# Long filters of a Hyena layer, transformed with the lags in eight residue classes of 128 instead of four of 256

## What is computed

```python
def hyena_filters(L, w1, b1, w2, b2, w3, b3, freq):
    ...
    h = (hid @ _f32(w3) + _f32(b3)).reshape(L, HY_ORDER, 2, HY_WIDTH)
    h = h * jnp.exp(-t * jnp.abs(deltas))[:, None, None, :]
    fwd, bwd = h[:, :, 0], h[:, :, 1]
    kern = jnp.concatenate([fwd, jnp.zeros((1, HY_ORDER, HY_WIDTH), jnp.float32), bwd[:0:-1]], axis=0)
    kern = kern / jnp.sum(jnp.abs(kern), axis=0, keepdims=True)
    return jnp.fft.rfft(kern, axis=0)

def long_conv(u, k_f, skip):
    L = u.shape[1]
    uf = _f32(u)
    y = jnp.fft.irfft(jnp.fft.rfft(uf, n=2 * L, axis=1) * k_f, n=2 * L, axis=1)[:, :L]
    return (y + uf * _f32(skip)).astype(u.dtype)
```

## Time and profile before

| what | value |
|---|---|
| median of three runs (lowest, highest) | 4657.28 us (4656.59, 4658.3) |
| the profiled execution, its own time | 4660.92 us |
| its span in the trace | 4658.4 us |
| TensorE (PE) busy | 4558.7 us, 98% |
| VectorE (DVE) busy | 2077.1 us, 45% |
| ScalarE (ACT) busy | 1006.0 us, 22% |
| GpSimd (POOL) busy | 44.8 us, 1% |
| granted TensorE clock, mean | 0.989 |

### The profile page before, as it was taken

The page is one execution under the profiler, slowest core; times in us unless marked ns, Lnnn a source line. Parts: engine busy times, 40 slices in busy tenths (PEclk is TensorE's granted clock), DMA queues, the critical chain, the costliest instruction groups (busy, mean ns, idle before and its releaser), DMA issues.

```text
span 4658.4 us, 39533 instructions
## 1 busy us (share of the span) xinstructions
PE 4558.7 (98%) x16516; PEld 2273.6 (49%) x16516; DVE 2077.1 (45%) x2485; ACT 1006.0 (22%) x1349; POOL 44.8 (1%) x35
## 2 busy tenths in 40 slices
PE   7999999998999999999999999999999999999998
PEld 3446666543444444554555554544444444444444
DVE  4555555224444477744344535323643362333412
ACT  3135555212111100002333222222310010000000
POOL 0000000000000000000000000000000000000000
PEclk9999999998999999999999999989999999999999
DMA  6200000211333422221111011112221221111211
GB/s 255 75 28 10 6 10 11 108 68 37 118 113 131 174 108 104 104 104 60 41 36 38 32 41 41 37 45 82 88 95 41 84 73 45 40 42 45 83 42 57
DMA packets 106813, 320.28 MB, mean 69 GB/s; under 512 B 26085, under 2 KB 44261, under 8 KB 99082
## 3 DMA queue, kind: packets, MB, share of 16 engines
q1 hardware_dynamic: 89708, 306.22, 18.6%
q10 hardware_dynamic: 16928, 11.54, 0.8%
HBM read 257.36 MB, written 60.36 MB: 68 GB/s over the span
## 4 chain that ended last, share of the span: by engine, by line
PE 70%; DVE 4%; issue 1%; DMA 0%; ACT 0%; POOL 0%; DVEq 0%; SPq 0%; POOLq 0%
PE late_dense L122 34%; PE late_four L3370 11%; PE late_two L3370 5%; PE late_four L1433 3%; PE late_four L3600 3%; PE late_four L2420 2%; PE late_dense L3600 2%; PE late_four L1445 1%; PE late_four L1450 1%; PE late_two L1625 1%; PE late_two L1631 1%; PE late_two L3600 1%; PE late_four L1649 1%; PE late_two L2774 0%; PE late_two L2776 0%
## 5 line engine op out<-in xcount | busy, mean ns | idle before, releaser
L122 PE MATMUL late_dense<-arena 128*128 128x512 f32 x4008 | 1764.7, 597 | 7.3 <-ACT arena L1758 2.9
L122 PEld LDWEIGHTS late_dense<-arena 128*128 128x128 f32 x4008 | 758.0, 191 | 934.9 <-issue 921.7
L3370 PE MATMUL late_four<-arena 128*128 128x512 f32 x1160 | 504.5, 592 | 0.0
L135 ACT ACTIVATE arena<-late_dense 128x512 f32<-128x512 f32 x198 | 118.0, 596 | 1112.5 <-PE late_dense L122 1084.6
L3370 PEld LDWEIGHTS late_four<-arena 128*128 128x128 f32 x1160 | 220.4, 190 | 277.4 <-issue 273.9
L122 PE MATMUL attn_dense<-arena 128*128 128x512 f32 x640 | 282.5, 599 | 4.0 <-ACT arena L637 2.1
L3370 PE MATMUL late_two<-arena 128*128 128x512 f32 x576 | 253.4, 592 | 0.0
L3419 DVE TENSOR_TENSOR arena<-late_four,arena 128x512 f32<-128x512 f32 x145 | 98.7, 689 | 299.3 <-PE late_four L3370 295.2
L839 PE MATMUL attn_dense<-matrices,arena 128*128 128x128 f32 x1280 | 187.6, 282 | 18.2 <-ACT arena L885 16.1
L122 PEld LDWEIGHTS attn_dense<-arena 128*128 128x128 f32 x640 | 121.7, 192 | 159.0 <-issue 154.4
L3370 PEld LDWEIGHTS late_two<-arena 128*128 128x128 f32 x576 | 109.4, 190 | 137.8 <-issue 136.3
(11 more groups left out here) (390 smaller groups left out, 4719.6 us busy)
## 6 DMA issues: line engine op xcount, KB each, us to landing
arena<-in_ada_w SPq DMA_DIRECT2D x12, 2048.0 KB, 8.1
arena<-in_w_ffn_in SPq DMA_DIRECT2D x44, 512.0 KB, 4.0
arena<-in_hy_tables SPq DMA_DIRECT2D x16, 1280.0 KB, 6.1
arena<-in_hy_w_in SPq DMA_DIRECT2D x32, 512.0 KB, 3.5
spectrum<-arena SPq DMA_DIRECT2D x8, 2048.0 KB, 8.0
arena<-spectrum SPq DMA_DIRECT2D x8, 2048.0 KB, 11.4
arena<-in_w_gates SPq DMA_DIRECT2D x32, 512.0 KB, 3.3
spill<-arena SPq DMA_DIRECT2D x26, 512.0 KB, 4.4
```

The costliest lines, as they stand in the source:

```text
L122: mm = pe.matmul(self.ps[:, n % SEG], self.wbuf[:, slot, k], job.rhs[:, k, cols], start=(job.first and k == 0), stop=(job.last and k == kt ...
L135: act.activation(job.out[:, cols], self.ps[:, n % SEG], job.func, scale=job.scale, bias=job.bias).then_inc(self.emptied[n % SEG], 1)
L3370: mm = pe.matmul(product_bank(M, name, i), left[:, k], right[:, k], start=(k == 0), stop=(k == 3))
```

## The change

The lags of the filters are ordered by residue modulo 8: eight classes of 128 lags, each one tile, and one tile of 128 base frequencies in place of two. For a base frequency the eight class results make eight frequencies, real and imaginary. Classes r and 8 - r (and 0 with 4, 2 with 6) are added in PSUM, with tables of both signs (`MINUS` lists the eight that are needed negated), so that each of four banks takes two matmuls. A step has four such groups of 8 matmuls (`filter_group_pe`): two on `minus`, which give the imaginary planes, then two on `plus` (the real ones). Each group is now read by `group_act` and `group_dve`, and `filter_spectrum_dve` joins the two groups of a part in eight planes; it has six instructions, two of them with the square root of one half. `n` counts these spectra as before, two a step, now by part and not by `f`. The store writes them back to the places that the signal part reads, in pieces of 512 numbers (2 KB). One table of 24 blocks of 128 by 128 (1.5 MB) is loaded once, ahead of the layer; the signal part's tables lose the negated part (1.25 MB to 1 MB), and the loads between filter steps fall away.

```diff
-            sp.dma_start(Y.tables.rearrange("p a b -> p (a b)")[:, 0:2 * L + BANK], A["hy_tables"][0]).then_inc(Y.early_in, 16)
+            sp.dma_start(Y.tables.rearrange("p a b -> p (a b)"), A["hy_filter_tables"]).then_inc(Y.early_in, 16)
...
+MINUS = ((COS, 4), (SIN, 7), (SIN, 6), (SIN, 5), (SIN, 4), (COS, 2), (COS, 1), (COS, 3))
+EVEN_LAGS = ((((COS, 4, 1), (COS, 0, 1)), ((COS, 4, -1), (COS, 0, 1)), ((COS, 2, 1), (COS, 6, 1)), ((SIN, 2, 1), (SIN, 6, -1))),
...
+def filter_group_pe(pe, Y, n, lags, rhs, fixed=0):
+    if n:
+        pe.wait_ge(Y.group_read, n)
+    for bank in (2, 3, 0, 1):
+        for at, (kind, r, sign) in enumerate(lags[bank]):
+            if fixed and bank == 0 and r == 0:
+                pe.wait_ge(Y.row_fixed, fixed)
+            mm = pe.matmul(Y.group[:, bank], filter_block(Y, kind, r, sign), rhs[:, r], start=(at == 0), stop=(at == 1))
     mm.then_inc(Y.group_filled, 1)
...
+def filter_spectrum_dve(dve, Y, n):
+    S, X, root = Y.S, Y.X, math.sqrt(0.5)
+    dve.wait_ge(Y.group_read, 2 * n + 2)
+    if n:
+        dve.wait_ge(Y.x_stored, 16 * n)
+    dve.tensor_tensor(X[:, 1], S[:, 5], S[:, 6], ALU.add)
+    dve.tensor_tensor(X[:, 3], S[:, 5], S[:, 6], ALU.subtract).then_inc(Y.d, 1)
+    dve.tensor_tensor(X[:, 0:4:2], S[:, 0:4:2], S[:, 4:8:3], ALU.add)
+    dve.tensor_tensor(X[:, 4:8:2], S[:, 0:4:2], S[:, 4:8:3], ALU.subtract)
+    dve.wait_ge(Y.d, 2 * n + 1)
+    dve.scalar_tensor_tensor(X[:, 5:8:2], X[:, 1:4:2], -root, S[:, 1:4:2], ALU.mult, ALU.add).then_inc(Y.d, 1)
+    dve.wait_ge(Y.d, 2 * n + 2)
+    dve.scalar_tensor_tensor(X[:, 1:4:2], X[:, 1:4:2], root, S[:, 1:4:2], ALU.mult, ALU.add).then_inc(Y.x_ready, 1)
...
         sp.wait_ge(Y.x_ready, n + 1)
-        sp.dma_start(A["spectrum"][n], Y.X).then_inc(Y.x_stored, 16)
+        it, real = divmod(n, 2)
+        dst = A["spectrum"][2 * it:2 * it + 2].rearrange("f p (s t) c -> t p s f c", t=2)[1 - real]
+        sp.dma_start(dst, Y.X.rearrange("p (s f) c -> p s f c", f=2)).then_inc(Y.x_stored, 16)
...
-        table(2 * it + 1)
         store_spectrum(2 * it)
         dense.load(sp, 4 * it + 4)
-        table(2 * it + 2)
+        if it == STEPS - 1:
+            table(0)
         store_spectrum(2 * it + 1)
...
             elif it:
-                pe.wait_ge(Y.x_ready, 2 * it)
+                pe.wait_ge(Y.group_read, 4 * it)
...
-        even_pe(pe, Y, 2 * it, Y.plus, Y.minus, it + 1)
+        filter_group_pe(pe, Y, 4 * it, EVEN_LAGS[1], Y.minus)
...
-        odd_lags_pe(pe, Y, 2 * it)
+        filter_group_pe(pe, Y, 4 * it + 1, ODD_LAGS[1], Y.minus)
...
-        even_pe(pe, Y, 2 * it + 1, Y.plus, Y.minus)
+        filter_group_pe(pe, Y, 4 * it + 2, EVEN_LAGS[0], Y.plus, it + 1)
         dense.multiply(pe, 1)
-        odd_lags_pe(pe, Y, 2 * it + 1)
+        filter_group_pe(pe, Y, 4 * it + 3, ODD_LAGS[0], Y.plus)
...
-        for f in range(2):
-            s = 2 * it + f
-            group_dve(dve, Y, s, 0)
-            if not f:
+        for real in range(2):
+            n = 2 * it + real
+            if n:
+                dve.wait_ge(Y.x_ready, n)
+            group_dve(dve, Y, 2 * n, 0)
+            if not real:
                 conv(4 * it)
-            if s:
-                dve.wait_ge(Y.x_stored, 16 * s)
-            dve.wait_ge(Y.group_filled, 2 * s + 2)
-            dve.wait_ge(Y.group_read, s + 1)
-            spectrum_dve(dve, Y, group[:, 0:2], group[:, 3:1:-1])
-            if not f:
+            group_dve(dve, Y, 2 * n + 1, 1)
+            filter_spectrum_dve(dve, Y, n)
+            if not real:
                 conv(4 * it + 1)
```

More of the change, by code:

```diff
@@ L1370, in __init__ @@
         self.ring, self.u, self.turned = rows[:, 17:19], rows[:, 19:21], rows[:, 21:23]
-        tables = self.tables = rows[:, 45:48].rearrange("p a b -> p (a b)")[:, 0:2 * L + BANK]
-        self.table = tables[:, 0:2 * L].rearrange("p (r s k c) -> p r s k c", r=CLASSES, s=2, k=2)
-        self.table_minus = tables[:, 2 * L:2 * L + BANK].rearrange("p (s k c) -> p s k c", s=2, k=2)
+        tables = rows[:, 45:48].rearrange("p a b -> p (a b)")
+        self.filter_table = tables.rearrange("p (n c) -> p n c", c=P)
+        self.tables = tables[:, 0:2 * L]
+        self.table = self.tables.rearrange("p (r s k c) -> p r s k c", r=CLASSES, s=2, k=2)
         self.plus, self.minus = pieces(23, 4), pieces(27, 4)
@@ L1411, in ring_row, with pair_pe @@
         return self.ring[:, self.ring_use[name] % 2]
-def even_pe(pe, Y, s, first, second, fixed=0):
-    if s:
[L1418 to L1431, removed]
+def pair_pe(pe, Y, s, odd, rhs):
+    pe.wait_ge(Y.table_in, 16 * (s + 1))
+    for a, r in enumerate((odd, odd + 2)):
+        for part in range(2):
             for k in range(2):
@@ L1435, in pair_pe, with filter_block, group_act @@
     mm.then_inc(Y.group_filled, 1)
[L1438 to L1451, removed]
+def filter_block(Y, kind, r, sign):
+    return Y.filter_table[:, LT * kind + r if sign > 0 else 2 * LT + MINUS.index((kind, r))]
+def filter_group_pe(pe, Y, n, lags, rhs, fixed=0):
[6 more added lines that the diff above has]
+            mm = pe.matmul(Y.group[:, bank], filter_block(Y, kind, r, sign), rhs[:, r], start=(at == 0), stop=(at == 1))
     mm.then_inc(Y.group_filled, 1)
-def group_act(act, Y, n, filled):
-    act.wait_ge(Y.group_filled, filled)
+def group_act(act, Y, n):
+    act.wait_ge(Y.group_filled, n + 1)
     if n:
@@ L1535, in hyena_sp @@
             at += 2
-        table(2 * STEPS + 2 * j + 1)
+        table(2 * j + 1)
         dense.load(sp, at)
@@ L1541, in hyena_sp @@
         if 2 * j + 2 < 8:
-            table(2 * STEPS + 2 * j + 2)
+            table(2 * j + 2)
         dense.load(sp, at + 3)
@@ L1691, in first_pair @@
         o, half = ROUNDS[j]
-        s, n, z = 2 * STEPS + 2 * j, 2 * STEPS + 4 * j, Y.z[half]
+        s, n, z = 2 * j, 4 * STEPS + 4 * j, Y.z[half]
         if o == 0:
@@ L1696, in first_pair @@
             pe.wait_ge(Y.inv_read, 8 * (half + 1))
-        pe.wait_ge(Y.group_read, n) if j else pe.wait_ge(Y.x_ready, s)
-        pair_pe(pe, Y, s, 0, z, z)
+        pe.wait_ge(Y.group_read, n)
+        pair_pe(pe, Y, s, 0, z)
     first_pair(0)
     for j, (o, half) in enumerate(ROUNDS):
-        s, n, z = 2 * STEPS + 2 * j, 2 * STEPS + 4 * j, Y.z[half]
+        s, n, z = 2 * j, 4 * STEPS + 4 * j, Y.z[half]
         dense.multiply(pe, 1)
         pe.wait_ge(Y.group_read, n + 1)
-        pair_pe(pe, Y, s, 1, z, z)
+        pair_pe(pe, Y, s, 1, z)
         dense.multiply(pe, 1)
@@ L1772, in hyena_act @@
             turn_act(act, Y, 4 * it - 1)
+        group_act(act, Y, 4 * it + 1)
+        if it:
             turn_act(act, Y, 4 * it)
@@ L3926, in hyena_arrays @@
     tokens = 4 * np.arange(LT // CLASSES * P).reshape(1, -1, P) + np.arange(CLASSES).reshape(-1, 1, 1)
-    by_class = tokens.reshape(-1)
-    angles = np.pi / L * np.multiply.outer(tokens, np.arange(2 * P) + 0.5)
+    shifted = np.concatenate([np.arange(P), 2 * P + np.arange(P)])
+    angles = np.pi / L * np.multiply.outer(tokens, shifted + 0.5)
     waves = np.stack([np.cos(angles), -np.sin(angles)], axis=1).astype(np.float32)
     tables = waves.reshape(CLASSES, 2, 2, P, 2, P).transpose(4, 3, 0, 1, 2, 5)
-    tables = np.concatenate([tables.reshape(2, P, -1), -tables[:, :, 3].reshape(2, P, -1)], axis=2)
+    eighths = LT * np.arange(P) + np.arange(LT).reshape(-1, 1)
+    by_class = eighths.reshape(-1)
+    angles = np.pi / L * np.multiply.outer(eighths, np.arange(P) + 0.5)
+    blocks = np.stack([np.cos(angles), -np.sin(angles)]).astype(np.float32)
+    minus = np.stack([-blocks[kind, r] for kind, r in MINUS])
+    filter_tables = np.concatenate([blocks.reshape(2 * LT, P, P), minus]).transpose(1, 0, 2)
     back_tables = waves.reshape(CLASSES, 2, 2 * P, 2, P).transpose(4, 3, 0, 1, 2).reshape(P, -1)
```

37 lines of the change are left out of this document (21 added, 16 removed).

## The result

| what | before | after |
|---|---|---|
| median of four runs (lowest, highest) | 4657.79 us (4656.59, 4659.83) | 4611.49 us (4610.95, 4615.45) |
| the profiled execution, its own time | 4660.92 us | 4615.45 us |
| its span | 4658.4 us | 4613.4 us |
| TensorE busy | 4558.7 us | 4511.3 us |
| VectorE busy | 2077.1 us | 2106.8 us |

The ratio is 0.9901, with a 95% interval of 0.9889 to 0.9912: 46.3 us faster, where 57.5 were forecast. The time, 4611.5, lies above the range that ended at 4608. VectorE gained 30 us of busy time and ScalarE 8, as the counts say (32 and 8 were forecast).

The account below looks back on a forecast made before the run. The prediction took TensorE as the bound, on the chain for 70% of the span. Removed matmuls (54.9 us) plus shorter table waits (2.6) made 57.5 us less, from 4657.3 to 4599.8 us, range 4596 to 4608.

Parts of the forecast that it names:

- The matmuls removed: Filter part's transform: 128 records of 0.429 us go over four steps, 54.9 us less, all on the path.
- The joins between groups: Between a step's filter groups: banks are free 3.6 us after a group, covers leave at least 3.3 us, cost nothing.
- the fear of one rival: In the spectrum on VectorE: strided instructions with a scalar might take longer than 1.28 us; chance 0.09.
- The work after the fourth group: Before the next step: spectrum ready at 10.0 us, VectorE starts the next filter pair 0.3 us late, cost nothing.
- The rival of VectorE late at a join: At filter group joins: TensorE waits for VectorE in every step, up to 43 us at stake; chance 0.09.
- its middle case of 4612: VectorE late at the filter joins, costing 3 us a step, gives 4612 us; chance 0.09.
- The tables: Signal part: loads shrink from 1280 to 1024 KB, three table waits lose 0.87 us each, 2.6 us together.
- The prediction's sentence on the Trainium skill: Signal part's tables: by the skill's 6.15 us for 1 MB, the smaller table lands no sooner and the waits stay.
- The stores: Spectrum stores in 2 KB pieces land in 8 to 13 us, within 21.8 us of room; slow-store rival (4702) 0.03.

Follow-up runs that it names:

- e4: Kernel before with half of the odd lags' transform matmuls left out (64 fewer), VectorE, ScalarE and loads unchanged, filters wrong: 4603.81 us.
- e8: Changed kernel with three quarters of `mix` made early and the last quarter left in its late place: 4614.09 us.
- e7: Kernel before, all matmuls kept, plus two unused VectorE additions (4.5 us) ahead of the second step's last spectrum: 4667.8 us.
- e3: Changed kernel with one more unused 128x1024 VectorE addition ahead of `mix` in its late place: 4614.34 us.
- e5: Changed kernel with `mix` moved early and the signal part's tables loaded at their old 1280 KB in place of 1024: 4605.3 us.

## Why the prediction was wrong

**The matmuls removed** were right: 128 records of 0.43 us went, 256 are left on one line, and e4, which leaves out as many and changes nothing else, is at 4603.8 against 4603 expected.

**The joins between groups** were right. VectorE's first sum of the third group waited 3.05 us for ScalarE's copy (2.5 forecast), the six instructions of a spectrum take 0.69, 0.68 and four times 1.22 us, the strided ones no longer than the others (the fear of one rival), and no group waited for its banks.

**The work after the fourth group** was the step that failed: the cover of 7.8 us between the fourth group and the next step's first matmul, costed at nothing. The prediction put a spectrum at 10.0 us after its group (9.6 measured, 1298.71 - 1289.10) and then let VectorE start the next step's decay products, of which TensorE asks for the result a dense tile later. It counted only what the step's loop showed and left out `mix`, which at the third step alone stands between the two, 2.35 us long, and which TensorE waits for *before* its first matmul of that step (`pe.wait_ge(Y.mixed, 2 * o)`). By the prediction's own numbers it would have been 10.0 + 2.35 = 12.4 us against a cover of 7.8, so 4.6 us late (4.05 measured). The trace of before showed it as two additions at 1321.31 that ended 0.7 us ahead of their use; with no wait to speak of behind them, they were in no list of waits.

**The rival of VectorE late at a join** had the right engine and, by its middle case of 4612, even the time, but another mechanism: 3 us in each of four steps for want of free banks. What happened was one wait in one step, for weights, and more than half of its cost was not waiting. That its time fits is luck.

**What a wait costs** was missing as a term. Every cover was priced as if losing it cost the microseconds by which it was short. At this place a lateness of 4 us cost 10.1. The trace of before had shown it, in the first step, at the waits of the earlier trace rows themselves:

```profile
1114.03 3.78 PE L1649 MATMUL late_four<-arena 65*128 65x512 f32 x4 [2.28 <-DVE arena L1846]
...
1124.97 9.06 PE L122 MATMUL late_dense<-arena 128*128 128x512 f32 x16 [2.89 <-ACT arena L1758]
```

Behind 2.28 us of waiting four records take 3.78 us in place of 1.88, and behind 2.89 us a dense tile takes 9.06 in place of 7.03 (granted clock 0.50 from 1114 to 1125). These waits follow one another too closely to read off what a single one costs, but they show that waits of this length can bring the clock down.

**The tables** were mis-sized: 2.6 us were forecast. The waits for them did fall, by 3.3 us in this trace (4.7 to 1.4; between 0.9 and 2.5 in the other traces with tables of the new size), and the landing's median from 6.1 to 5.5:

```profile
DMA to landing us min/median/max: 4.6/5.5/7.3
```

But 1.65 us in the three rounds together was all that VectorE's chain allowed, and the last round's 0.76 of that was lost at the inverse transform. From the second round's first pair to where the last inverse transform goes on it takes 338.10 us (1613.24 to 1951.34), and 338.77 before (1657.99 to 1996.76), so that 0.7 us were left. Then the wait of 2.40 us there, in place of 1.74 and 0.26, brought the clock down in the changed kernel's trace: from its end to the next dense tile it takes 29.00 us in place of 27.84. The whole signal part, from its first pair to that dense tile, takes 450.92 us after (1529.42 to 1980.34) and 450.43 before (1574.17 to 2024.60): no gain at all. The prediction's sentence on the Trainium skill ("DMA: Bandwidth & Descriptors", Bandwidth), with its 6.15 us for 1 MB, did not help either way. That figure is for transfers issued from GpSimd, and these are issued from SyncE: 1 MB landed in 4.6 to 7.3 us here. To read the earlier trace rows as "within 5.7 to 6.1" was wrong as well, since these are the lowest and the median, and the highest is 8.5.

**The stores** were right: 2 MB in pieces of 2 KB land like whole ones (7.4 to 8.8 before), and nothing waited for them.

```profile
DMA to landing us min/median/max: 8.0/8.1/9.0
```

**Sum.** The forecast was 57.5 us less. Of these 10.1 come back at the third step, 2.6 do not come from the tables, and 0.5 are lost there instead: 57.5 - 10.1 - 3.1 = 44.3, against 45.0 in the two profiled spans and 46.3 between the medians. The rest is within what runs of one kernel differ.

## What to carry to other kernels

When work is added to an engine off the critical path, list all that is queued behind it on that engine up to the next thing the bound engine needs, for each pass of the loop and not for the typical one; an item that ends just ahead of its use shows in no list of waits. Price a lost cover on TensorE as the lateness plus what the clock takes, and look for that price in the trace of before, behind waits of like length: at the third step it was next to nothing with 1.55 us of idleness, and 5 to 7 us on top with 2.27 to 5.07. And where a wait is shortened, measure from one meeting point of the two engines to the next: a second engine's chain of fixed length takes the gain back.

## What the runs showed of the hardware

The granted clock falls from 1.00 to 0.50, that is from 2.4 to 1.2 GHz, after a single idle stretch of TensorE (3.94 us in the changed kernel), though the engine was busy for all of the 38 us from 1252 to 1290 and again right after the wait. The Trainium skill ("TensorE: Matmul & The Clock Gate", Part 1: The HAM clock gate) names these two levels; the rows agree. The length of the idle stretch alone does not settle it. At the third step 2.27 us were enough (e8). In e7 a wait of 1.99 us for a table was enough:

```profile
1942.29 8.80 PE L1433 MATMUL late_four<-arena 128*128 128x512 f32 x16 [1.99 <-DMA arena<-in_hy_tables]
```

There the sixteen records take 8.80 us in place of 7.1. Waits of 1.94 and 2.12 us in e4, on the other hand, had no low clock behind them. The same wait of 2.4 us before the last inverse transform brought the clock down in eight traces of ten and not in two (e3 and e5). After the change:

```profile
1951.30:1955.00 3.70, 3.66 (x9) 2.95 (x10) 3.50 (x4) 0.00 (x0) 0.00 (x0) 0.54 0.00 0
1955.00:1960.00 5.00, 5.00 (x25) 4.41 (x24) 3.07 (x3) 0.00 (x0) 0.00 (x0) 1.00 0.26 105
```

and in e3, after the same wait:

```profile
1951.90:1956.00 4.10, 4.01 (x19) 3.55 (x20) 3.90 (x5) 0.00 (x0) 0.00 (x0) 1.00 0.00 0
```

The low stretch there cost about 1.2 us (29.00 against 27.84), at the third step 5 to 7. Why one is so much shorter stays open, and so does what besides the length decides whether the clock falls.
